# Expert rows gathered once per column, with u and v side by side, in a ring of eight places of 8 KB

## The reference

```
s = einsum('thpd,hpnd->thpn', q, peer_sub_keys);  sv, si = top_k(s, 16)
cand = sv[:, :, 0, :, None] + sv[:, :, 1, None, :];  cv, ci = top_k(cand, 16)
e = (first index) * 128 + (second index)               # (token, 8 heads, 16)
g = softmax(cv)
act = gelu(einsum('td,thkd->thk', xb, peer_u[e]))      # a dot product with row u of each expert
out = einsum('thk,thkd->td', g * act, peer_v[e])       # a weighted sum of the rows v
```

## Time and profile before

| | before |
|---|---|
| median of 3 runs | 2368.91 us (2366.36 to 2372.15) |
| span of the profiled execution | 2346.3 us |
| its own time beside the span | not given by the page |
| PE busy | 1763.5 us (75%), x8918 |
| DVE busy | 1610.7 us (69%), x3641 |
| POOL busy | 1234.0 us (53%), x1251 |
| ACT busy | 989.6 us (42%), x1711 |
| DMA | 695.64 MB, mean 296 GB/s |

### The profile page before, as it was taken

How to read it: one execution, slowest core, us unless ns; L and a number is a source line. 1 busy time by engine, 2 the same in 40 slices (tenths; PEclk the granted TensorE clock), 3 DMA queues, 4 the chain that set the end, 5 groups by cost and what they waited for, 6 DMA issues and landing times.

```text
span 2346.3 us, 26214 instructions
## 1 busy us (share of the span) xinstructions
PE 1763.5 (75%) x8918; PEld 1299.5 (55%) x8918; DVE 1610.7 (69%) x3641; ACT 989.6 (42%) x1711; POOL 1234.0 (53%) x1251
## 2 busy tenths in 40 slices
PE   7995999638858967987877977847876976753556
PEld 3553657327646756665655755636654655543445
DVE  2546682887876777778676786786887778677441
ACT  1223343133544323555665664643342443233345
POOL 1000000367666666666667666656566656767664
PEclk9997799858977857978978987977987887875667
DMA  7001202499998989999999999979899889999997
GB/s 256 24 11 38 56 1 73 156 354 405 351 342 331 346 312 353 354 359 370 344 361 392 372 354 385 344 262 389 314 354 376 314 325 348 373 401 348 358 372 283
DMA packets 191573, 695.64 MB, mean 296 GB/s; under 512 B 26192, under 2 KB 28624, under 8 KB 188368
## 3 DMA queue, kind: packets, MB, share of 16 engines
q0 software_dynamic: 178608, 674.33, 76.2%
q1 hardware_dynamic: 12832, 19.65, 2.8%
HBM read 690.14 MB, written 3.76 MB: 296 GB/s over the span
## 4 chain that ended last, share of the span: by engine, by line
PE 42%; DVE 21%; issue 12%; POOL 6%; ACT 6%; another core or an unknown queue 5%; DVEq 4%; DMA 4%; ACTq 0%; POOLq 0%
PE ps L2230 8%; PE ps L2037 7%; DVE region L1690 6%; POOL region L682 6%; DVEq L1097 4%; DVE xall L1701 3%; DMA region<-in_peer_v,region 3%; PE ps L1722 2%; ACT region L1086 2%; PE ps L2054 2%; PE ps L1987 2%; PE ps L2130 1%; PE ps L2019 1%; PE ps L2082 1%
## 5 line engine op out<-in xcount | busy, mean ns | idle before, releaser
L682 POOL DMA_INDIRECT region<-in_peer_u,region x507 | 515.7, 1017 | 611.6 <-DVEq L1097 440.1
L2230 PE MATMUL ps<-ident,region 128*128 128x128 f32 x3312 | 552.7, 325 | 262.4 <-issue 138.1
L682 POOL DMA_INDIRECT region<-in_peer_v,region x571 | 571.7, 1001 | 335.2 <-issue 145.8
L1690 DVE SCALAR_TENSOR_TENSOR region<-region,h_now 128x1024 f32<-128x1024 f32 x507 | 611.7, 1214 | 116.5 <-DMA region<-in_peer_u,region 69.6
L2230 PEld LDWEIGHTS ps<-ident,region 128*128 128x128 f32 x3312 | 472.1, 169 | 350.6 <-issue 204.3
L1086 ACT ACTIVATE region<-region 128x1024 f32<-128x1024 f32 x414 | 464.9, 1139 | 245.0 <-DMA region<-in_peer_v,region 189.0
L2037 PE MATMUL ps<-w_uk_s,region 128*128 128x512 f32 x544 | 294.3, 669 | 8.7 <-issue 6.7
L1701 DVE SCALAR_TENSOR_TENSOR xall<-region,xall 128x1024 f32<-128x1024 f32 x157 | 201.7, 1285 | 20.9 <-issue 4.7
L2037 PEld LDWEIGHTS ps<-w_uk_s,region 128*128 128x128 f32 x544 | 106.3, 218 | 91.8 <-issue 88.2
L946 ACT ACTIVATE region<-ps 128x512 f32<-128x512 f32 x136 | 80.2, 590 | 163.5 <-PE ps L2037 101.3
L953 ACT ACTIVATE region<-ps 128x256 f32<-128x256 f32 x136 | 51.5, 379 | 202.2 <-remote 115.0
(11 more groups left out here) (404 smaller groups left out, 2824.5 us busy)
## 6 DMA issues: line engine op xcount, KB each, us to landing
region<-in_w_peer_q POOLq DMA_DIRECT2D x31, 512.0 KB
region<-in_peer_v,region POOLq DMA_INDIRECT x571
region<-in_peer_u,region POOLq DMA_INDIRECT x507
region<-in_w_in POOLq DMA_DIRECT2D x8, 882.0 KB, 14.8
region<-in_w_peer_q SPq DMA_DIRECT2D x8, 512.0 KB, 4.7
region<-in_x_turned SPq DMA_DIRECT2D x5, 512.0 KB, 3.5
region<-in_w_out SPq DMA_DIRECT2D x2, 1024.0 KB, 12.4
region<-in_w_out SPq DMA_DIRECT2D x1, 2048.0 KB, 18.3
```

Source lines behind the costliest of these rows:

```text
L682: pool.indirect_dma_start(ring[r][:], None, table, bass.IndirectOffsetOnAxis(ap=experts[:, t, n:n + 1], axis=0)).then_inc(landed[r], 16)
L1690: v.scalar_tensor_tensor(ring[r][:], ring[r][:], 1.0, h_now[:], ALU.mult, ALU.mult, accum_out=acts[:, t % 2, n:n + 1]).then_inc(S["u_done" ...
L2230: last = te.matmul(ps[6 + c // 4][:, (c % 4) * P:(c % 4 + 1) * P], ring[r][:, c * P:(c + 1) * P], ident[:], is_transpose=True, start=(m == ...
```

## The change

One input array peer_rows takes the place of peer_u and peer_v: row e is row e of u followed by row e of v, 8 KB (put together on the host, as an input). One gather per column brings both, and the ring has eight places of 8 KB. A place is held until the column's v is added. Additions follow two steps behind the dots on ScalarE and VectorE (ADD_LAG) and three on TensorE (PE_LAG) instead of 22 and 23. Gelu and gates are made for two columns at a time, ahead of the first one's addition. Since the sums of a tile are now taken out shortly before the next one's begin, the first four columns of tiles 1 to 3 (HEAD) are added by VectorE, and so are the first four columns of all, until the PSUM banks are free at step 6. VectorE adds 156 columns in all. Chunks of weights pass two to a place. The normalised tokens of tiles 1 to 4 have a place in `tables`.

```diff
-        LAG = 22
-        GRP = 16
+        ADD_LAG, PE_LAG = 2, 3
...
-        STEPS = NCOLS + LAG + 4
+        STEPS = NCOLS + PE_LAG + 4
...
+        MIXED_AT = 6
+        SHARES = [(0, MIXED_AT, 1, 1), (38, 54, 3, 4), (100, 160, 2, 3), (167, 184, 1, 2), (258, 275, 1, 2), (362, 480, 3, 5), (480, 496, 1, 2)]
+        HEAD = 4
...
         def on_dve(m):
-            k = m + LAG
+            if P <= m < SEQ and m % P < HEAD:
+                return True
+            k = m + ADD_LAG
...
-        AHEAD = NRING // 2 - 1
+        AHEAD = NRING - 1
...
-        for k in range(NCOLS + LAG):
+        for k in range(NCOLS):
             beside[len(fetched)] = pages[k]
             fetched += weights[k]
-            if k < NCOLS:
-                fetched.append(("u", *tile_of(k)))
-            if k >= LAG:
-                fetched.append(("v", *tile_of(k - LAG)))
+            fetched.append(("e", *tile_of(k)))
...
-                    if kind_ == "u":
-                        pool.wait_ge(S["u_done"], x + 1)
-                    elif kind_ != "v":
+                    if kind_ != "e":
                         pool.wait_ge(S["w_used"], weights_used(fetched[f - NRING]))
                     elif on_dve(x):
                         pool.wait_ge(S["v_mixed"], x - pe_rows(x) + 1)
                     else:
                         pool.wait_ge(S["v_added"], pe_rows(x) + 1)
...
-                    table = a["peer_u"] if kind == "u" else a["peer_v"]
-                    pool.indirect_dma_start(ring[r][:], None, table, bass.IndirectOffsetOnAxis(ap=experts[:, t, n:n + 1], axis=0)).then_inc(landed[r], 16)
+                    pool.indirect_dma_start(ring[r][:], None, a["peer_rows"], bass.IndirectOffsetOnAxis(ap=experts[:, t, n:n + 1], axis=0)).then_inc(landed[r], 16)
...
-                m = k - LAG
-                if k % GRP == 1 and 1 < k <= NCOLS + 1:
-                    j = k // GRP - 1
-                    act.wait_ge(S["dotted"], j + 1)
-                    t, n = tile_of(GRP * j)
-                    sc(acts[:, t % 2, n:n + GRP], acts[:, t % 2, n:n + GRP], ACT.Gelu_apprx_tanh).then_inc(S["gelu"], 1)
+                m = k - ADD_LAG
                 if 0 <= m < NCOLS:
                     t, n = tile_of(m)
-                    if m % GRP == 0:
-                        act.wait_ge(S["wts"], m // GRP + 1)
-                    r = place_of["v", t, n]
+                    r = place_of["e", t, n]
+                    if n % 2 == 0:
+                        pair = acts[:, t % 2, n:n + 2]
+                        act.wait_ge(S["dotted"], m + 2)
+                        sc(pair, pair, ACT.Gelu_apprx_tanh).then_inc(S["gelu"], 1)
                     if not on_dve(m):
-                        act.wait_ge(landed[r], landing["v", t, n])
-                        sc(ring[r][:], ring[r][:], ACT.Copy, scale=wts[:, t % 2, n:n + 1]).then_inc(S["v_scaled"], 1)
+                        act.wait_ge(S["wts"], m // 2 + 1)
+                        sc(ring[r][:, D:W], ring[r][:, D:W], ACT.Copy, scale=wts[:, t % 2, n:n + 1]).then_inc(S["v_scaled"], 1)
...
-                m = k - LAG
+                m = k - ADD_LAG
+                if 0 <= m < NCOLS and m % 2 == 0:
+                    t, n = tile_of(m)
+                    dve.wait_ge(S["gelu"], m // 2 + 1)
+                    v.tensor_tensor(wts[:, t % 2, n:n + 2], acts[:, t % 2, n:n + 2], gates[:, t, n:n + 2], ALU.mult).then_inc(S["wts"], 1)
```

107 lines of the change are left out of this document (55 added, 52 removed).

## The result

The changed kernel takes 2217.2 us (median of 4 runs, 2207.74 to 2223.7) against 2370.07 us for the kernel before in the same session: ratio 0.935, 95% interval 0.9324 to 0.9376. The experiments add a condition that changes what this means: on other chips the same change makes the kernel slower.

What follows compares the result with a forecast made beforehand. Issue and transfer of gathers were taken as nearly the same bound, with no engine full and delays never caught up. Terms +14, -33, -8, -45, +18, +25 gave -29: span 2317, time 2340 us, range 2275 to 2410.

Steps and rivals of the forecast that it cites:

- Filling the pipeline: Start of the table: first columns now need 8 KB rows, dot 39 near 557 us; +14 us, bounds +5 and +28.
- Draining it: After the last dot: 46.2 us shrink to about 13, no 22 v columns left; -33 us, bounds -25 and -35.
- Bigger rows: Supply-bound columns: 8 KB rows take 2.55 us per column instead of 2.63; -8 us, ends 0 and -25.
- Gelu and gates per pair: VectorE and ScalarE: 288 of each instead of 36, ten more table loads; +18 us, ends +5 and +70.
- Supply in the middle: Middle stretch: one gather refills places at once, v lands with u, half the waits won; -45 us, ends 0 and -89.
- the sign that I named for it: Middle stretch: no wait of ScalarE for peer rows, and VectorE's wait for them under 25 us.
- Engines tied together: Sixteen sampling stages: additions can no longer run in bursts beside VectorE's other work; +25 us, ends 0 and 83.
- the lockstep: Rival, sampling bursts, gelu and gates: all 83 us of the stages fall on the path, 2398 us; chance 0.26.
- places held too long: Rival, ring: TensorE late by over two steps lets the queue run dry, 2390 us; chance 0.08.
- The test named for the lockstep: VectorE's wait for gelu and ScalarE's for gates together over 100 us, TensorE idle beside, would prove the forecast wrong.
- 22.6 us around the span: Whole kernel: difference between median 2368.91 and span 2346.3 us, taken as time outside the span and added to the forecast.
- the much faster rival: Nearly everywhere: supply was the bound, middle 220 us shorter at 407 GB/s, a third of it gives 2267 us; chance 0.15.

Runs made afterwards that it cites:

- e1: Changed kernel with each place filled by two gathers of 4 KB rows, u and v: 2369.2 us, kernel before 2368.9 (first kind of chip).
- e3: Changed kernel with a second gather of 64 bytes per partition behind each column's, awaited by the dot: 2355.8 us, kernel before 2368.9 (first kind).
- s1: Kernel before with gelu and gates for two columns instead of sixteen, without VectorE's drain ahead; additions still 22 steps behind: 2369.7 us, kernel before 2347.9 (first kind).
- r5: Changed kernel with two gathers of 4 KB rows per place, repeated on another chip of the first kind: 2357.6 us, kernel before 2347.9.
- e5: Changed kernel with ADD_LAG 3 and PE_LAG 4 instead of 2 and 3: 2299.4 us, kernel before 2368.9 (first kind).
- e4: Changed kernel gathering only the 4 KB u rows, v left out of the computation: 2108.8 us, kernel before 2368.9 (first kind).
- s2: Kernel before with gelu and gates per pair, no VectorE drain ahead, additions 6 steps behind dots instead of 22: 2344.3 us, kernel before 2347.9 (first kind).
- s3: Kernel before with gelu and gates for eight columns, no VectorE drain ahead, additions 12 steps behind dots: 2340.9 us, kernel before 2347.9 (first kind).
- e6: Changed kernel with a ring of seven places instead of eight: 2283.6 us, kernel before 2138.8 (second kind of chip).
- e8: Changed kernel with PE_LAG 2 instead of 3: 2383.1 us, kernel before 2138.8 (second kind).
- e9: Changed kernel with gelu and gates for one column at a time, ADD_LAG 1 and PE_LAG 2: 2306.7 us, kernel before 2138.8 (second kind).

## Why the prediction was wrong

**Filling the pipeline, +14: right.** Dot 39 came at 556.0, forecast 557. On the second kind of chip it costs 30 us (526.3 to 556.6), a little over the upper bound of 28: there the kernel before keeps the queue full at this stage too.

**Draining it, -33: right.** 46.3 to 13.2 us; 39.4 to 12.8, only 27, on the second kind.

**Bigger rows, -8: right in rate.** 415 GB/s per full share make 2.53 us per column, forecast 2.55, and a gather of GpSimd takes 0.987 us (L689 x576), forecast 1.0. e1 against e3 puts some 13 us on it, not clear of noise. The lower end was added up wrongly: half of 576 columns at 0.16 us are 46 us, not 25.

**Gelu and gates per pair, +18: nothing against its size.** s1 measured 14 us, 5 to 23, in the kernel before on the first kind, where something else sets the time. 33 table loads in place of 24 were at gelu, 1283 ns each, and 73 in place of 62 in all, where I had ten more. The Trainium skill ("ScalarE: Activation LUTs", "What ACT_TABLE_LOAD costs") gives 2.66 us for a load with its drain; the 1283 ns agree with its load alone, and no run here shows the drain or separates the eleven loads. The whole of s1, which has these loads too, costs no more than 23 us, waits and gates included.

**Supply in the middle, -45 with ends 0 and -89: the step that failed.** All terms for the middle (-8, -45, +18, +25) came to -10 us; it became shorter by 110. The edit that this term is about, one gather in place of two, is what r5 and e1 take back: their middle is 118 and 147 us longer than that of the changed kernel, so one gather brought that much where supply and bigger rows together had 53 and could not exceed 114 by their ends. The ceiling of 89 us was the sum of TensorE's and VectorE's waits for rows. Those rows did not say what I took from them, nor did the sign that I named for it: VectorE's wait for rows was to be under 25 us and is 120.9 in the faster kernel. The same program on the second kind of chip shows 387 us of ScalarE's wait for v and 154 of VectorE's for u. In the trace that the prediction rests on, there is another sort of wait in their place, whose releaser the profile doesn't name ("remote": the semaphore's event is there, but no recorded work that raises it ended near it). The kernel before, 500 to 2100 us:

```profile
ACT region L953 <- remote: 115.0, 33, 8.5
...
POOL region L682 <- remote: 85.1, 48, 3.8
...
ACT region L1033 <- remote: 41.3, 9, 11.9
```

None of them is in the trace of the changed kernel, on the same kind of chip, and none in that of the kernel before on the second kind, where the first is only this:

```profile
ACT region L953 <- PE ps L2028: 75.3, 40, 8.7
```

e3, after the change plus a small gather, has them again on the first kind (its L690 is the gather, L962 what L953 is before):

```profile
POOL region L690 <- remote: 60.8, 33, 3.3
ACT region L962 <- remote: 53.8, 19, 7.3
```

So has every kernel with two gathers per column there: 183 to 427 us of such waits between 500 and 2100 us over all engines (374 in the kernel before), against none in the changed kernel and e5 and 3 in e4. The page of before also gives its v gathers no time to landing, the last number of such a row. First the kernel before as the prediction had it, then the same on the second kind:

```profile
region<-in_peer_v,region POOLq DMA_INDIRECT x571
```

```profile
region<-in_peer_v,region POOLq DMA_INDIRECT x571, 11.6
```

So records of landings were missing there (its trace holds 10653 landing events, that of the same program on the second kind 21360), and a wait for a DMA could not always be booked as one. The changed kernel's page on the first kind lacks that number too, with 10992 landing events of the 11856 that its trace on the second kind has. The missing number alone is therefore no sign of the stalls, but it says that some waits for DMA may not be counted.

How such a wait looks in the timeline of before:

```profile
1251.15 1.13 ACT L1086 ACTIVATE region<-region 128x1024 f32<-128x1024 f32 x1
...
1251.30 0.27 PE L2028 MATMUL ps<-ident,region 128*32 128x128 f32 x1
...
1258.65 0.39 ACT L953 ACTIVATE region<-ps 128x256 f32<-128x256 f32 x1 [6.37 <-remote]
1258.74 0.94 POOL L682 DMA_INDIRECT region<-in_peer_v,region  x1 [3.81 <-remote]
```

TensorE's transpose is over at 1251.57 and ScalarE's own work at 1252.28, but ScalarE copies it out at 1258.65, and GpSimd starts again within 0.1 us of it. The semaphore events of the trace tell what both waited for: TensorE. The event that ends ScalarE's wait is that of this transpose, at 1258.62, and GpSimd's semaphore counts TensorE's additions; its events come at 1258.48, 1258.57 and 1258.72, while the last addition before them ended at 1253.42. So the word of finished work reached the others five to seven us late and all at once. (Ends of matmuls are modelled; it may be that TensorE really ended late.) The transfers went on meanwhile; of 1252 to 1258.5 us:

```profile
1252.00:1258.50 6.50, 1.09 (x8) 0.86 (x8) 5.02 (x8) 0.28 (x1) 2.32 (x3) 0.69 1.03 411
```

This is no single case. Between 500 and 2100 us, 209 of the 720 recorded semaphore events of TensorE in the kernel before come more than 1.5 us after the last instruction that raises that semaphore, half of them 2.9 us or more, the latest 14.9. In the other kernels with two gathers on the first kind it is 122 to 223. It is none of 844 in the changed kernel there, none in e5, two (at 1.6 us) in e4, and none in any kernel on the second kind. The events of ScalarE and VectorE are late at most twice in a trace.

Why TensorE's events are late is not settled. It needs two gathers (or one and a small one) per column, it does not need their bytes, it exists on one kind of chip and not on the other. Whether it comes from GpSimd's issue, from the number of landings, from a dot's wait for a second landing, or from the recording itself, which loses events there and goes along with every timed run, stays open: the runs that were to tell the others apart fell on the second kind of chip, and for the recording there was none. Nor did any run measure how much of the 110 us such delays make.

**Engines tied together, +25, and the slower rivals.** On the first kind s2 and s3 show no cost of short distances, but there something else sets the time. On the second kind the middle is 76 us longer after the change, and the total 83. Both slower rivals (2398 for the lockstep, 2390 for places held too long, +29 and +21 over before) name what is left as the loss there, which is larger than I priced them together. The forecast's sentence that holding the u half "costs nothing of its own", because of two steps in reserve, is wrong: one place of the eight is worth 63 us (e6, second kind). The test named for the lockstep, over 100 us of VectorE's wait for gelu and ScalarE's for gates, came out at 367 us on the first kind (60.4 and 306.8) in a kernel that was 153 us faster; it says that the engines are tied, not that they lost by it.

**22.6 us around the span.** Also wrong. The profiled execution after takes 2218.07 us with a span of 2216.0: 2 us lie around it. In every timed execution on record the time is 1.7 to 3.0 us over the span, so the span of 2346.3 belongs to an execution of some 2349 us, faster than the timed ones (2366 to 2372), and what I took for overhead was the distance between them. It made the predicted time some 20 us too long; the middle made it 100 us too long, and these two are nearly the whole error of 123 us.

**A reading.** The issue before each gather, 145.8 over 571, is 0.26 us and not 0.27, which changes nothing. The 2 us per DMA that the prediction takes from the Trainium skill stand in "DMA: Bandwidth & Descriptors" under "Anatomy of one DMA — SWDGE (gpsimd) path"; under "Bandwidth" is the advice on 1 MiB.

**The chain and the shares.** "A delay in one is never caught up" was the right reading of the earlier trace rows, and it spoke for the much faster rival, which I gave 0.15 because of VectorE's "mere 25 us for u rows". That rival was nearest, but its reason (the queue at its full rate nearly everywhere) is not what happened. From 500 to 2000 us, first before, then after:

```profile
500.00:2000.00 1500.00, 1167.83 (x6278) 885.85 (x6277) 1133.26 (x2231) 706.24 (x1187) 971.35 (x969) 0.81 0.93 351
```

```profile
500.00:2000.00 1500.00, 1181.27 (x6597) 903.66 (x6595) 1215.86 (x2584) 784.48 (x1449) 531.53 (x544) 0.84 0.95 378
```

The share went from 0.93 to 0.95 only, but the rate by 8%. Divided by the share, before moved 377 GB/s and after 398, so a share near 1 in the earlier trace rows did not say that the queue ran at its full 399.

## What to carry to other kernels

Before a wait's total is used as the ceiling of a gain, see whether the trace can book such waits at all: gathers without a time to landing and engines idle for 5 to 15 us behind "remote" are signs that it may not, and then the gap between the queue's full rate and its mean (here 407 and 352 GB/s, 220 us of the middle) is the safer ceiling: 110 came of it. A rate is divided by the share of busy time before a queue is called full. A span is set against the same execution's own time, never against a median. And joining two gathers halves their number but ties two lifetimes into one place: with eight places held to the end, one place was worth 3% here and one step of distance, either way, 4% to 7%, and the version that wins on one chip can be the slower one on the next, so both are timed on more than one.

## What the runs showed of the hardware

- One program's time depends on the chip, or on something else that goes with the session, and the other's doesn't: the kernel before takes 2370, 2369 and 2348 us in three sessions and 2139, 2137 and 2139 in three others; the changed kernel 2217 and 2220. Every kernel with two gathers per column took 2341 to 2370 us on the first kind, whatever its lags.
- While the queue is full, transfers run alike on both: 399 GB/s per full share and, on the second kind, also 399 (20.12 MB in 50 us at 100.8%). Rows of 8 KB move 415 on both. Over 500 to 2000 us the kernel before moves 377 per full share on the first kind and 393 on the second.
- With two gathers per column on the first kind, 122 to 223 of some 700 recorded semaphore events of TensorE come over 1.5 us late, and half or more of the landing events are missing (10653 of 21360 in the kernel before, 9080 of 21016 in e3, against the same programs on the second kind); with one gather none to two are late, and 7% of the landing events are missing in the changed kernel. On the second kind none is late.
- Issuing a gather of 128 rows costs GpSimd about 1.0 us, whether its rows have 4 KB (1.017 and 1.001), 8 KB (0.987) or 16 KB (0.950). A gather of 4 KB rows of v lands 11.6 us after its issue in the median and one of 8 KB rows 9.3 (second kind, whole span). The Trainium skill ("DMA: Bandwidth & Descriptors", "Anatomy of one DMA — SWDGE (gpsimd) path") has 2 us fixed plus the bytes, which the prediction estimates at 3.2 and 4.4 us; no run here shows a gather in an empty queue against one in a full one, so that the rest is queueing is likely but not shown.
- The mean granted clock differs between kernels on the same chip: 0.84 in the changed one (2220 us), 0.82 in e8 (2383 us) and 0.81 in e9 (2307 us), so it does not follow the time alone.
